# Two norms at the entry of the first FFN and of the SSD mixer: another order of weight splits, multiplications and additions

## The chip, the core and the metric

The kernel runs on one core of a Trainium2 chip. The metric is the device time of one execution, in microseconds (us). TensorE is called PE in the rows, VectorE DVE, ScalarE ACT, GpSimd POOL, SyncE SP.

## What is computed

Two layers over 256 context and 256 latent tokens of width 1024: the first has latent attention and a SwiGLU FFN, the second a bidirectional Mamba-2 (SSD) mixer and a SwiGLU FFN. Each of the four stands behind an RMS norm with modulation. What matters here is the entry of the first FFN and that of the SSD mixer:

```python
x = x + mod_x[2] * out_x
hx = rms_norm(x, norm_ffn[i]) * (1.0 + mod_x[4]) + mod_x[3]
x = x + mod_x[5] * swiglu(hx, ffn_w1[i], ffn_w3[i], ffn_w2[i])
...
def rms_norm(x, g):
    xf = x.astype(jnp.float32)
    y = xf * lax.rsqrt(jnp.mean(xf * xf, axis=-1, keepdims=True) + EPS)
    return (y * g.astype(jnp.float32)).astype(x.dtype)
```

The context tokens go through the same with their own modulation.

## The kernel before

**Layout.** The stream `X` ("residual") stands transposed: 1024 features as eight blocks k of 128 partitions, 512 tokens on the free axis, columns 0 to 255 the context, 256 to 511 the latent tokens (`HALF`). A matmul has a weight block as its stationary side and tokens as its moving side.

**Split numbers.** Each float32 operand of a matmul is cut into a high and a low half (fp32r), and a product is three matmuls: low tokens by high weights, high by high, high by low weights (lines 1776 to 1778). Weights come in blocks n of 128x1024. SyncE loads block n into one of four buffers `raw` once the low half of block n-4, which held the same buffer, has been made. `hi(n)` on ScalarE (L632) copies the raw block into `w_hi`, once the block is loaded and TensorE has used up block n-4, which held the same buffer . `lo(n)` on DVE (L1160) subtracts: `w_lo` = raw - `w_hi`; it waits for `w_hi`. The blocks have running numbers: `WO` the attention's output projection (8), `F0` the first FFN's w1 and w3, `G0` its w2 (three blocks an output tile, `g0(m)`), `BC` and what follows the SSD's input projection.

**Order.** Each engine runs its program in the order written; nothing is reordered. Semaphores join the engines. A wait stops all that is queued behind it on its engine.

**The two entries.** `norm_halves(w, n, ...)` exists twice, on ScalarE and on DVE, with w = 3 for the first FFN (called with n = F0 + 1) and w = 4 for the SSD mixer (n = BC + 1). It makes the norm and the operand for the context tokens first (half 0), then for the latent ones (half 1), while TensorE still ends the last tiles of the product before: in the first case output tiles 5, 6 and 7 of the projection (`SPLIT[3]`), in the second tile 7 of the FFN's w2 (`SPLIT[4]`), each done for the context columns first and for the latent columns afterwards. `add_half` (L1404) takes such a tile out of its PSUM bank: X = X + gate * bank. `square_half` (L662) squares it, POOL has summed the tiles before, and `half_sum` on TensorE (L1829, L1832) adds over the partitions with a matrix of ones. `rms_half` (L668) takes the square root, `inverse` (L1416) the reciprocal.

Of the operand's eight blocks k the even ones come as `value(h, k)` on DVE (L1424: X * gain * reciprocal), the high half with the shift on ScalarE (L677), and `low(h, k)` on DVE (L1434). The odd ones come from POOL (L502: X * reciprocal), ScalarE (L681 gain and shift, L683 high half) and `low(h, k)` (L1432). The buffers of `value` and of POOL hold two blocks each: value 4 waits for low 0's count, POOL's k = 5 for that of low 1, k = 7 for that of low 3.

TensorE takes the operand in four passes, of 48 matmuls each:

```python
def half_pair(w, n, outs, hh_, hl_, h):
    _, c0, c1 = HALF[h]
    pe.wait_ge(w_lo, n + 2)
    for k in range(KD):
        pe.wait_ge(h_lo, 8 * (2 * (w - 3) + h) + k + 1)
...
def four_halves(w, n, outs, hh_, hl_):
    half_pair(w, n, outs[0:2], hh_, hl_, 0)
    half_sum(w, 1)
    if w == 3:
        pe.wait_ge(added, 10)
    half_pair(w, n + 2, outs[2:4], hh_, hl_, 0)
    half_pair(w, n, outs[0:2], hh_, hl_, 1)
    half_pair(w, n + 2, outs[2:4], hh_, hl_, 1)
```

So the first pass wants blocks n and n+1 of the weights (F0 and F0+1, BC and BC+1), the second n+2 and n+3; `lo` of the first of them, F0 or BC, is made ahead of `norm_halves`. SyncE's first load of the FFN's following blocks waits for all sixteen low halves (`h_lo` 16), since vectors are loaded beside them into buffers that the norm uses.

Of the kernel before, what the change touches and what calls it, by code (L numbers as in the profile page):

```python
# [167 lines left out]
def late(t, k):  # L168

    return t >= k if isinstance(t, int) else True  # L170


def program(nc, a, out):
# [9 lines left out]
    with ExitStack() as fixed:  # L183
# [3 lines left out]
        def sem(name):  # L187
            return fixed.enter_context(nc.semaphore(name))
# [119 lines left out]
        w_hi, w_lo, w_used = sem("w_hi"), sem("w_lo"), sem("w_used")  # L308
# [312 lines left out]
        def _(act):  # L621
            A = nc.scalar.activation

            def hi(n, s):

                if isinstance(n, int) and n >= NBLK:
                    return
                act.wait_ge(raw_loaded[s % RING], 4 * (n - s % RING) + 16)
                if late(n, RING):
                    act.wait_ge(w_used, n - RING + 1)  # L630
                c = COLS[s]
                A(wh[s % RING][:, 0:c], raw[s % RING][:, 0:c], ACT.Copy).then_inc(w_hi, 1)  # L632
# [25 lines left out]
            def square_half(w, i, m, h, count):  # L658

                act.wait_ge(added, count)  # L660
                _, c0, c1 = HALF[h]
                A(T[:, SQ_AT[w, m], c0:c1], X[:, m, c0:c1], ACT.Square).then_inc(h_sq, 1)  # L662

            def rms_half(w, h):

                _, c0, c1 = HALF[h]
                act.wait_ge(h_sum, 2 * (w - 3) + h + 1)
                A(T[:, 4, c0:c1], bank[6 + h][:, 0:256], ACT.Sqrt, bias=eps[:, 0:1], scale=1.0 / D).then_inc(h_root, 1)  # L668

            def his_half(w, h, ks, hdst, gn, shift):  # L670

                m, c0, c1 = HALF[h]
                b = 2 * (w - 3) + h
                for k in ks:
                    if k % 2 == 0:
                        act.wait_ge(h_nv, 4 * b + k // 2 + 1)
                        A(hdst[:, k, c0:c1], T[:, 2 + k // 2 % 2, c0:c1], ACT.Identity, bias=shift(k, m)).then_inc(h_hi, 1)  # L677
                    else:
                        act.wait_ge(h_nx, 4 * b + k // 2 + 1)
                        v = T[:, 6 + k // 2 % 2, c0:c1]  # L680
                        A(v, v, ACT.Identity, bias=shift(k, m), scale=gn(k, m)).then_inc(h_odd, 1)  # L681
                        act.wait_ge(h_odd, 4 * b + k // 2 + 1)
                        A(hdst[:, k, c0:c1], v, ACT.Copy).then_inc(h_hi, 1)  # L683

            def norm_halves(w, n, base, hdst, gn, shift):

                S = len(SPLIT[w])
                for i, m in enumerate(SPLIT[w]):
                    square_half(w, i, m, 0, base + i + 1)
                hi(n, n)  # L690
                if S == 3:
                    square_half(w, 0, 5, 1, base + 4)
                rms_half(w, 0)
                his_half(w, 0, (0, 1), hdst, gn, shift)
                if S == 3:
                    square_half(w, 1, 6, 1, base + 5)
                hi(n + 1, n + 1)
                his_half(w, 0, (2, 3), hdst, gn, shift)
                square_half(w, S - 1, 7, 1, base + 2 * S)
                hi(n + 2, n + 2)  # L700
                his_half(w, 0, (4, 5, 6, 7), hdst, gn, shift)
                rms_half(w, 1)
                his_half(w, 1, range(KD), hdst, gn, shift)

# [189 lines left out]
            for m in range(5):  # L894
                hi(WO + m + RING, WO + m + RING)
                squares(3, m, 0, 0)
            norm_halves(3, F0 + 1, 5, H0h, lambda k, m: gain[1][:, k, m:m + 1], lambda k, m: mod[0][:, 24 + k, m:m + 1])

            def hidden(j, g, u, nt, U, n, s):
# [16 lines left out]
            for m in range(7):  # L916
                for n in range(g0(m), g0(m + 1)):
                    hi(n + RING, n + RING)
                squares(4, m, ADD1, 0)
            act.wait_ge(mod_done, 4)  # L920
            norm_halves(4, BC + 1, ADD1 + 7, H1h, lambda k, m: gain[2][:, k, m:m + 1], lambda k, m: mod[1][:, k, m:m + 1])
            act.wait_ge(up_zero, 4)

# [192 lines left out]
            for m in range(1, 8):  # L1116
                if m in (1, 2, 4, 5):
                    n = SO + 12 + (1, 2, 4, 5).index(m)
# [32 lines left out]
        def _(dve):  # L1151
            V = nc.vector

            def lo(n, s):

                if isinstance(n, int) and n >= NBLK:
                    return
                dve.wait_ge(w_hi, n + 1)
                c = COLS[s]
                V.tensor_tensor(wl[s % RING][:, 0:c], raw[s % RING][:, 0:c], wh[s % RING][:, 0:c].bitcast(f32), SUB).then_inc(w_lo, 1)  # L1160
# [239 lines left out]
            def add_half(ready, count, m, o, h, layer, chunk):  # L1400

                dve.wait_ge(ready, count)
                src, c0, c1 = HALF[h]
                V.scalar_tensor_tensor(X[:, m, c0:c1], o[:, 0:256], mod[layer][:, 8 * chunk + m, src:src + 1],  # L1404
                                       X[:, m, c0:c1], MUL, ADD).then_inc(added, 1)

            def norm_halves(w, n, base, lat_outs, used, gn, hdst, ldst, shift):

                S = SPLIT[w]
                layer, chunk = 0, 2 if w == 3 else 5  # L1410

                def inverse(h):

                    _, c0, c1 = HALF[h]
                    dve.wait_ge(h_root, 2 * (w - 3) + h + 1)
                    V.reciprocal(T[:, 5, c0:c1], T[:, 4, c0:c1]).then_inc(h_inv, 1)  # L1416
                    dve.wait_ge(h_inv, 2 * (w - 3) + h + 1)

                def value(h, k):

                    m, c0, c1 = HALF[h]
                    if k >= 4:
                        dve.wait_ge(h_lo, 8 * (2 * (w - 3) + h) + k - 3)
                    V.scalar_tensor_tensor(T[:, 2 + k // 2 % 2, c0:c1], X[:, k, c0:c1], gn(k, m), T[:, 5, c0:c1], MUL, MUL).then_inc(h_nv, 1)  # L1424

                def low(h, k):

                    m, c0, c1 = HALF[h]
                    dve.wait_ge(h_hi, 8 * (2 * (w - 3) + h) + k + 1)
                    hk = hdst[:, k, c0:c1].bitcast(f32)  # L1430
                    if k % 2:
                        V.tensor_tensor(ldst[:, k, c0:c1], T[:, 6 + k // 2 % 2, c0:c1], hk, SUB).then_inc(h_lo, 1)  # L1432
                    else:
                        V.scalar_tensor_tensor(ldst[:, k, c0:c1], T[:, 2 + k // 2 % 2, c0:c1], shift(k, m), hk, ADD, SUB).then_inc(h_lo, 1)  # L1434

                if len(S) == 3:
                    add_half(w_used, used, 5, lat_outs[0], 1, layer, chunk)
                dve.wait_ge(added, base + len(S))
                inverse(0)
                value(0, 0)  # L1440
                value(0, 2)
                if len(S) == 3:
                    add_half(w_used, used + 1, 6, lat_outs[1], 1, layer, chunk)
                low(0, 0)
                low(0, 1)
                lo(n, n)
                value(0, 4)
                low(0, 2)
                low(0, 3)
                lo(n + 1, n + 1)  # L1450
                add_half(w_used, used + 2, 7, lat_outs[-1], 1, layer, chunk)
                value(0, 6)
                low(0, 4)
                low(0, 5)
                lo(n + 2, n + 2)
                low(0, 6)
                low(0, 7)
                dve.wait_ge(added, base + 2 * len(S))
                inverse(1)
                value(1, 0)  # L1460
                for k in range(0, KD, 2):
                    if k + 2 < KD:
                        value(1, k + 2)
                    low(1, k)
                    low(1, k + 1)
# [8 lines left out]
            for i, m in enumerate(SPLIT[3]):  # L1474
                add_half(half_out, i + 1, m, bank[1 + i], 0, 0, 2)
            norm_halves(3, F0 + 1, 5, (bank[4], bank[5], bank[0]), WO + 6, lambda k, m: gain[1][:, k, m:m + 1],
                        H0h, H0l, lambda k, m: mod[0][:, 24 + k, m:m + 1])

# [24 lines left out]
            for m in range(7):  # L1503
# [9 lines left out]
                if m == 5:  # L1513
                    bias(1, 0, 48, VEC)
                    gains(2, 1, 1, "norm_mix", vec_bias, 4, 3)
                    gains(3, 1, 4, "norm_ffn", vec_bias, 4, 4)
            add_half(half_out, 4, 7, bank[1], 0, 0, 5)
            norm_halves(4, BC + 1, ADD1 + 7, (bank[2],), g0(7) + 1, lambda k, m: gain[2][:, k, m:m + 1],
                        H1h, H1l, lambda k, m: mod[1][:, k, m:m + 1])

# [927 lines left out]
```

## Time and profile before

| what | before |
|---|---|
| median of three runs | 1218.68 us (1218.53 to 1220.82) |
| time of the profiled execution | 1220.89 us |
| span of the profiled execution | 1219.1 us |
| PE busy | 1155.3 us (95%) |
| DVE busy | 866.8 us (71%) |
| ACT busy | 636.0 us (52%) |
| POOL busy | 216.4 us (18%) |

The span goes from the first to the last instruction; the time has in addition what lies around it, here 1.8 us. Busy shares are means over stages with different limits: PE is busy nearly always, and what it waits for at the entries of the stages is to be read there. Times in the rows are in us from the span's start.

### The profile page before, as it was taken

How to read it: one execution, taken by the hardware profiler on the slowest of the kernel's cores; microseconds unless marked ns; L12 is line 12 of the kernel's file. 1: busy time of each engine (PE TensorE's matmuls, PEld its weight loads, DVE VectorE, ACT ScalarE, POOL GpSimd, SP SyncE). 2: the span in 40 equal slices, each digit the busy share in tenths (PEclk: the TensorE clock that was granted, in tenths of full speed). 3: DMA queues.
4: the chain of work that ended last, by engine and by line, in shares of the span. 5: the costliest groups of instructions: out<-in, count | busy, mean ns of one | idle time of the engine just before them, and what ended most of it. 6: DMA issues, size and time to landing. Idle time of an engine off the chain costs nothing.

```text
span 1219.1 us, 19185 instructions
## 1 busy us (share of the span) xinstructions
PE 1155.3 (95%) x6954; PEld 968.7 (79%) x6954; DVE 866.8 (71%) x1320; ACT 636.0 (52%) x1078; POOL 216.4 (18%) x162
## 2 busy tenths in 40 slices
PE   5799999988999999999999899999999899999996
PEld 3577676668988888888888888887777799999996
DVE  0896889876687777776664688785788666767654
ACT  3646888644432223232222487567777356676742
POOL 0201445422100000000111200033965210000010
PEclk9899999999999999999999999999999899999999
DMA  9534132141375556546443132222212344555562
GB/s 379 203 122 138 53 104 87 36 163 45 125 256 185 177 189 206 170 178 208 144 160 123 53 130 87 82 76 85 66 58 69 105 139 157 174 171 175 167 213 65
DMA packets 48178, 168.27 MB, mean 138 GB/s; under 512 B 5232, under 2 KB 6512, under 8 KB 47856
## 3 DMA queue, kind: packets, MB, share of 16 engines
q1 hardware_dynamic: 48112, 167.38, 41.2%
q8 instruction: 42, 0.69, 0.2%
q14 instruction: 24, 0.20, 0.0%
HBM read 166.31 MB, written 1.05 MB: 137 GB/s over the span
## 4 chain that ended last, share of the span: by engine, by line
PE 73%; DVE 11%; ACT 6%; issue 6%; DMA 1%; SPq 1%; POOL 1%; DVEq 0%; ACTq 0%
PE bank L1776 21%; PE bank L1778 21%; PE bank L1777 21%; DVE w_lo L1160 3%; ACT w_hi L632 3%; PE bank L2212 2%; PE bank L2224 2%; DMA raw<-in_w_in 1%; PE bank L2245 1%; DVE softmax_max L1331 1%; PE bank L2234 1%; ACT L1135 1%; DVE mla_h_lo L1351 1%; PE bank L2139 1%; DVE vec_weights L1237 1%
## 5 line engine op out<-in xcount | busy, mean ns | idle before, releaser
L1160 DVE TENSOR_TENSOR w_lo<-raw,w_hi 128x1024 fp32r<-128x1024 f32 (+1 forms) x226 | 274.6, 1218 | 132.8 <-ACT w_hi L632 132.5
L632 ACT ACTIVATE w_hi<-raw 128x1024 fp32r<-128x1024 f32 (+1 forms) x226 | 230.2, 1021 | 243.3 <-PE bank L1778 219.2
L1776 PE MATMUL bank<-ffn_h_lo,w_hi 128*128 128x258 f32 (+2 forms) x736 | 246.1, 334 | 6.3 <-DVE ffn_h_lo L1434 2.8
L1778 PE MATMUL bank<-ffn_h_hi,w_lo 128*128 128x258 f32 (+2 forms) x736 | 244.3, 332 | 0.0
L1777 PE MATMUL bank<-ffn_h_hi,w_hi 128*128 128x258 f32 (+2 forms) x736 | 244.3, 332 | 0.0
L1776 PEld LDWEIGHTS bank<-ffn_h_lo,w_hi 128*128 128x128 f32 x736 | 139.3, 189 | 23.0 <-DVE ffn_h_lo L1434 3.3
L1777 PEld LDWEIGHTS bank<-ffn_h_hi,w_hi 128*128 128x128 f32 x736 | 139.1, 189 | 14.5
L1778 PEld LDWEIGHTS bank<-ffn_h_hi,w_lo 128*128 128x128 f32 x736 | 138.9, 189 | 14.7
L484 POOL TENSOR_TENSOR scratch<-scratch 128x512 f32<-128x512 f32 (+1 forms) x24 | 33.7, 1406 | 619.2 <-ACT scratch L641 619.2
L1776 PE MATMUL bank<-ssd_h_lo,w_hi 128*128 128x256 f32 (+2 forms) x360 | 125.7, 349 | 4.2 <-DVE ssd_h_lo L1434 2.3
L1776 PE MATMUL bank<-ffn_hidden_lo,w_hi 128*128 128x256 f32 (+1 forms) x374 | 123.4, 330 | 1.1 <-DVE ffn_hidden_lo L1730 0.9
L1778 PE MATMUL bank<-ffn_hidden_hi,w_lo 128*128 128x256 f32 (+1 forms) x374 | 123.1, 329 | 0.0
L1777 PE MATMUL bank<-ffn_hidden_hi,w_hi 128*128 128x256 f32 (+1 forms) x374 | 122.6, 328 | 0.0
L1777 PE MATMUL bank<-ssd_h_hi,w_hi 128*128 128x256 f32 (+2 forms) x360 | 117.3, 326 | 0.0
L1778 PE MATMUL bank<-ssd_h_hi,w_lo 128*128 128x256 f32 (+2 forms) x360 | 117.1, 325 | 0.0
L1535 DVE SCALAR_TENSOR_TENSOR scratch<-conv_in,par,scratch 128x512 f32<-128x512 f32 (+1 forms) x96 | 73.5, 767 | 18.4 <-ACT scratch L943 15.8
L1776 PEld LDWEIGHTS bank<-ssd_h_lo,w_hi 128*128 128x128 f32 (+1 forms) x360 | 68.0, 189 | 14.6 <-issue 3.9
L1776 PEld LDWEIGHTS bank<-ffn_hidden_lo,w_hi 128*128 128x128 f32 x374 | 70.3, 188 | 8.7 <-DVE ffn_hidden_lo L1730 1.1
L1777 PEld LDWEIGHTS bank<-ffn_hidden_hi,w_hi 128*128 128x128 f32 x374 | 70.7, 189 | 7.0
L1778 PEld LDWEIGHTS bank<-ffn_hidden_hi,w_lo 128*128 128x128 f32 x374 | 70.1, 188 | 7.0
L1777 PEld LDWEIGHTS bank<-ssd_h_hi,w_hi 128*128 128x128 f32 (+1 forms) x360 | 68.1, 189 | 9.4 <-issue 3.6
L1237 DVE SCALAR_TENSOR_TENSOR matvec_products<-scratch,silu_c_rows 128x1024 f32<-128x1024 f32 x56 | 73.8, 1317 | 0.0
(275 smaller groups left out, 2180.0 us busy)
## 6 DMA issues: line engine op xcount, KB each, us to landing
raw<-in_w SPq DMA_DIRECT2D x120, 512.0 KB, 4.4
scratch<-in_vec_w SPq DMA_DIRECT2D x56, 512.0 KB, 3.6
vec_weights<-in_vec_w SPq DMA_DIRECT2D x24, 512.0 KB, 3.6
raw<-in_w_xbc SPq DMA_DIRECT2D x24, 512.0 KB, 3.5
ada_start<-in_ada_w SPq DMA_DIRECT2D x8, 1024.0 KB, 17.2
raw<-in_w_z SPq DMA_DIRECT2D x16, 512.0 KB, 3.5
raw<-in_w_so SPq DMA_DIRECT2D x16, 512.0 KB, 3.5
raw<-in_w SPq DMA_DIRECT2D x16, 384.0 KB, 4.4
```

The source lines that it names most:

```text
L484: nc.gpsimd.tensor_tensor(T[:, ACC[w], 0:n], before, T[:, (b + k) % 2, 0:n], ADD).then_inc(sq_used, 2 if k == 1 else 1)
L632: A(wh[s % RING][:, 0:c], raw[s % RING][:, 0:c], ACT.Copy).then_inc(w_hi, 1)
L1135: A(T[:, u, 0:LAT], T[:, 6 + u, 0:LAT], ACT.Silu, bias=shift_out[:, u, 0:1]).then_inc(silu_done, 1)
L1160: V.tensor_tensor(wl[s % RING][:, 0:c], raw[s % RING][:, 0:c], wh[s % RING][:, 0:c].bitcast(f32), SUB).then_inc(w_lo, 1)
L1237: V.scalar_tensor_tensor(dst, buf, 1.0, crow[:, s, :], MUL, MUL, accum_out=m).then_inc(done, 1)
L1331: V.tensor_reduce(mx[:, c], bank[p][:, :], AX.X, ALU.max).then_inc(maxed, 1)
L1535: V.scalar_tensor_tensor(acc, up[:, u, seg, r:r + 256], par[:, PAR["conv_w"] + 5 * t + r:PAR["conv_w"] + 5 * t + r + 1], acc, MUL, ADD).th ...
L1776: mm(o, lh, rl, start=first, stop=False)
L1777: mm(o, lh, rh, start=False, stop=False)
L1778: return mm(o, ll, rh, start=False, stop=final)
L2212: last = mm(bank[6 + b][:, :], tabv(("gt", "lt")[d_]), mask_at(d_)[:, 4 * b:4 * b + 4, :], start=d_ == 0, stop=d_ == 1)
L2224: mm(bank[s // 2][:, :], Bt[:, tt, g, :], xsf[i % 6], start=s != 1, stop=s != 0).then_inc(st_mm, 1)
```

## The change

On ScalarE, the high half of weight block n+1 is made directly behind the square root of half 0, ahead of all high halves of the operand; that of n+2 behind the operand's k = 5; the squares of tiles 6 and 7 of half 1 stand later in the row of the operand's blocks (behind k = 3 and at the end). On DVE, the low half of block n is made ahead of the reciprocal; the operand's values 4 and 6 stand ahead of the additions of tiles 6 and 7 of half 1, the low half of block n+1 behind value 6, that of n+2 behind the last low half of the operand. Half 1 is left as it is. The block numbers are F0+1, F0+2, F0+3 in the first FFN and BC+1, BC+2, BC+3 in the SSD mixer; there, with `S == 1`, the additions and squares of tiles 5 and 6 don't exist. The same instructions run as before.

```diff
@@ ScalarE, norm_halves
                 rms_half(w, 0)
-                his_half(w, 0, (0, 1), hdst, gn, shift)
+                hi(n + 1, n + 1)
+                his_half(w, 0, (0, 1, 2, 3), hdst, gn, shift)
                 if S == 3:
                     square_half(w, 1, 6, 1, base + 5)
-                hi(n + 1, n + 1)
-                his_half(w, 0, (2, 3), hdst, gn, shift)
+                his_half(w, 0, (4, 5), hdst, gn, shift)
+                hi(n + 2, n + 2)
+                his_half(w, 0, (6, 7), hdst, gn, shift)
                 square_half(w, S - 1, 7, 1, base + 2 * S)
-                hi(n + 2, n + 2)
-                his_half(w, 0, (4, 5, 6, 7), hdst, gn, shift)
                 rms_half(w, 1)
@@ DVE, norm_halves
                 dve.wait_ge(added, base + len(S))
+                lo(n, n)
                 inverse(0)
                 value(0, 0)
                 value(0, 2)
-                if len(S) == 3:
-                    add_half(w_used, used + 1, 6, lat_outs[1], 1, layer, chunk)
                 low(0, 0)
                 low(0, 1)
-                lo(n, n)
                 value(0, 4)
                 low(0, 2)
                 low(0, 3)
+                if len(S) == 3:
+                    add_half(w_used, used + 1, 6, lat_outs[1], 1, layer, chunk)
+                value(0, 6)
                 lo(n + 1, n + 1)
-                add_half(w_used, used + 2, 7, lat_outs[-1], 1, layer, chunk)
-                value(0, 6)
                 low(0, 4)
                 low(0, 5)
-                lo(n + 2, n + 2)
+                add_half(w_used, used + 2, 7, lat_outs[-1], 1, layer, chunk)
                 low(0, 6)
                 low(0, 7)
+                lo(n + 2, n + 2)
```

## Rows read from the trace of the kernel before

**Rows 1.** Waits of PE from 298 us on, longest group: total, times, longest.

```profile
PE bank L1776 <- DVE w_lo L1160: 4.5, 3, 1.8
```

**Rows 2.** Timeline of PE, first FFN's entry: start, duration, line, operands, idle before.

```profile
294.87 0.28 PE L1778 MATMUL bank<-mla_h_hi,w_lo 128*128 128x256 f32 x1
...
297.71 0.28 PE L1778 MATMUL bank<-mla_h_hi,w_lo 128*128 128x256 f32 x1
298.97 0.39 PE L1776 MATMUL bank<-ffn_h_lo,w_hi 128*128 128x256 f32 x1 [0.98 <-DVE w_lo L1160]
...
304.42 0.39 PE L1776 MATMUL bank<-ffn_h_lo,w_hi 128*128 128x256 f32 x1 [2.35 <-DVE ffn_h_lo L1434]
...
306.83 0.58 PE L1776 MATMUL bank<-ffn_h_lo,w_hi 128*128 128x256 f32 x1 [0.41 <-DVE ffn_h_lo L1434]
...
309.48 0.59 PE L1829 MATMUL bank<-scratch,ones 128*128 128x256 f32 x2
...
311.02 0.47 PE L1776 MATMUL bank<-ffn_h_lo,w_hi 128*128 128x256 f32 x1
```

**Rows 3.** Timeline of DVE, context half of the same entry.

```profile
292.93 1.75 DVE L1416 RECIPROCAL scratch<-scratch 128x256 f32<-128x256 f32 x1 [1.82 <-ACT scratch L668]
294.72 1.94 DVE L1424 SCALAR_TENSOR_TENSOR scratch<-residual,gain,scratch 128x256 f32<-128x256 f32 x2
...
297.71 1.21 DVE L1160 TENSOR_TENSOR w_lo<-raw,w_hi 128x1024 fp32r<-128x1024 f32 x1
```

**Rows 4.** Timeline of ACT, context half of the same entry.

```profile
290.69 1.06 ACT L632 ACTIVATE w_hi<-raw 128x1024 fp32r<-128x1024 f32 x1 [1.96 <-PE bank L1778]
...
292.35 0.48 ACT L668 ACTIVATE scratch<-bank,eps 128x256 f32<-128x256 f32 x1 [0.30 <-PE bank L1832]
295.82 0.51 ACT L677 ACTIVATE ffn_h_hi<-scratch,mod 128x256 fp32r<-128x256 f32 x1 [2.99 <-DVE scratch L1424]
...
302.09 0.42 ACT L662 ACTIVATE scratch<-residual 128x256 f32<-128x256 f32 x1 [2.22 <-DVE residual L1404]
...
305.71 0.42 ACT L683 ACTIVATE ffn_h_hi<-scratch 128x256 fp32r<-128x256 f32 x1
```

**Rows 5.** Timeline of DVE, latent half of the same entry.

```profile
313.77 1.94 DVE L1424 SCALAR_TENSOR_TENSOR scratch<-residual,gain,scratch 128x256 f32<-128x256 f32 x2
...
316.35 0.43 DVE L1432 TENSOR_TENSOR ffn_h_lo<-scratch,ffn_h_hi 128x256 fp32r<-128x256 f32 x1 [0.24 <-ACT ffn_h_hi L683]
316.69 0.48 DVE L1424 SCALAR_TENSOR_TENSOR scratch<-residual,gain,scratch 128x256 f32<-128x256 f32 x1
317.09 0.96 DVE L1434 SCALAR_TENSOR_TENSOR ffn_h_lo<-scratch,mod,ffn_h_hi 128x256 fp32r<-128x256 f32 x1
```

**Rows 6.** Timeline of POOL, one multiplication of each half.

```profile
297.86 1.65 POOL L502 TENSOR_TENSOR scratch<-residual,scratch 128x256 f32<-128x256 f32 x1 [1.48 <-DVE ffn_h_lo L1432]
...
316.86 0.91 POOL L502 TENSOR_TENSOR scratch<-residual,scratch 128x256 f32<-128x256 f32 x1 [1.43 <-DVE ffn_h_lo L1432]
```

**Rows 7.** Timeline of PE, the SSD's entry.

```profile
678.55 0.39 PE L1776 MATMUL bank<-ssd_h_lo,w_hi 128*128 128x256 f32 x1 [1.77 <-DVE w_lo L1160]
...
684.00 0.38 PE L1776 MATMUL bank<-ssd_h_lo,w_hi 128*128 128x256 f32 x1 [2.34 <-DVE ssd_h_lo L1434]
...
688.75 0.59 PE L1829 MATMUL bank<-scratch,ones 128*128 128x256 f32 x2
```

**Rows 8.** Timelines of ACT and DVE, the SSD's entry.

```profile
671.05 1.06 ACT L632 ACTIVATE w_hi<-raw 128x1024 fp32r<-128x1024 f32 x1 [1.91 <-PE bank L1778]
...
672.57 1.75 DVE L1416 RECIPROCAL scratch<-scratch 128x256 f32<-128x256 f32 x1 [3.94 <-ACT scratch L668]
```

**Rows 9.** Busy us (instructions) by engine of two stretches; then granted PE clock, DMA.

```profile
304.40:309.40 5.00, 4.57 (x24) 4.17 (x25) 2.29 (x4) 1.70 (x4) 0.00 (x0) 0.66 0.00 0
...
684.00:688.70 4.70, 4.70 (x24) 4.42 (x25) 2.29 (x4) 1.68 (x4) 0.00 (x0) 0.64 0.35 119
```

**Rows 10.** Timeline of DVE, first split behind the first FFN's entry.

```profile
325.61 1.23 DVE L1160 TENSOR_TENSOR w_lo<-raw,w_hi 128x1024 fp32r<-128x1024 f32 x1 [4.68 <-ACT w_hi L632]
```

## The prediction

> **What bounds the kernel now.** I read the waits of TensorE first: behind 298 us the list is short, and at its head stands DVE's split of a weight block (w_lo), 4.5 us in three waits [rows 1]. In the two stages of the change TensorE waits for that and for DVE's low half of the operand (ffn_h_lo, ssd_h_lo) alone [rows 2, 7]. Then TensorE's own timeline through the first FFN's entry [rows 2]. Its last output-projection matmul starts at 297.71; the first FFN matmul stands 0.98 us later, released by w_lo (block F0+1); after four of eight k it waits 2.35 us for the low half of k=4, after k=6 another 0.41 us; the half sum of the latent tokens starts at 309.48 and the next pair at 311.02. From 306.83 on its timeline shows no wait before the SSD's entry at 678.55. So what is taken off this entry is kept: everything behind it hangs on TensorE, or on the operand that the entry makes. Behind the SSD's entry too the list has no wait for a split or an operand until the second FFN. The SSD's entry has the same waits, 1.77 and 2.34 us, and its half sum starts at 688.75 [rows 7].
>
> Why the low halves are late is read from DVE and ScalarE. DVE idles 1.82 us ahead of the first reciprocal and then puts the block F0+1 (1.21 us) between the low halves of k=1 and k=2 [rows 3]. ScalarE makes F0+1's high half already at 290.69, and idles 2.99 us ahead of the first high half at 295.82 [rows 4]. Two gaps stand ahead of the operand, and weights are made inside it.
>
> **The change part by part, first FFN.** No instruction is added or dropped; only orders change, on ScalarE and DVE. Nothing moves on SyncE or POOL, but their waits on w_lo and h_lo follow.
>
> *lo(F0+1) ahead of the reciprocal.* Its high half ends at 290.69 + 1.06 = 291.75; the split takes 1.21 us [rows 3], so until about 293.0. The reciprocal started at 292.93, after the square root at 292.35 + 0.48 [rows 3, 4]. Cost 0 to 0.1 us: the gap covers it. Without the gap it would cost 1.2. Queued behind it is everything of this half, and the square root's result waits with it.
>
> *hi(F0+2) behind the square root.* It needs the projection's tile m=6, whose last matmul ends at 294.87 + 0.28 = 295.15 [rows 2]. It runs about 295.25 to 296.20, where the first high half stood at 295.82 [rows 4]: that moves by 0.38 us, and the low halves with it. This is the one new cover that doesn't quite fit.
>
> *The order of the operand.* DVE now does value 0, 2, low 0, 1, value 4, low 2, 3, value 6, low 4, as it does already for the latent half; so I take the latent half's rhythm [rows 5]: from the first value low 1 starts at +2.58 (316.35 - 313.77), and low 2 ends 1.70 behind that start (317.09 + 0.96 - 316.35). With values at 294.72 as before and 0.38 for ScalarE: low 1 starts at 297.68, low 2 ends at 299.38, low 3 at 299.7. Ahead of low 4 then stand add_half (0.4), value 6 (0.4 alone, 0.9 beside a POOL multiplication), lo(F0+2) (1.2, with the start of the next inside it 1.1) and low 4 itself (0.48): 299.7 + 0.4 + 0.9 + 1.1 + 0.5 = 302.6.
>
> *What TensorE sees.* A matmul is 0.118 us (24 of them from 294.87 to 297.71), one k of a pair of tiles is six, 0.71 us [rows 2]; a start after a wait costs 0.1 more. F0+1 is there at 293, low 0 at 297.2, so the pair starts at 297.83 instead of 298.97. k=2 waits 0.2 (low 2 at 299.38), k=4 would start at 300.95 and waits 1.6 until 302.6. Thereafter ScalarE decides: the square, hi(F0+3) and four high halves, the same six pieces as now from 302.09 to 305.71 + 0.42, take 4.04 us [rows 4], now from 300.15: 304.2. Low 7 is done at 304.65 and TensorE reaches k=7 at 304.8: no further wait. The pair ends and the half sum starts at 305.5; before 309.48. **Gain 4.0 us.** Of it about 1.2 is the clock: before, the stretch 304.4 to 309.4 has a granted mean of 0.66 [rows 9], a part of it at 1.2 instead of 2.4 GHz, right behind the 2.35 us wait; from 306.83 the two k left would have taken 1.5 at the full clock, to 308.3.
>
> *lo(F0+3) at the end.* It now ends after low 7, near 305.8; the second pair needs it when the half sum is done, 305.5 + 1.54 = 307.0 (309.48 to 311.02). Margin 1.2 us, cost nothing. The square of m=7 ends at 304.5, a microsecond ahead of the half sum. From there on all is as before, 4.0 us earlier. SyncE's next weight load waits for the last low half of the latent half, which follows the half sum; its split starts at 325.61 [rows 10] and ends at 326.8, and TensorE asks for it after 144 matmuls from 311.02, at 328.1: 1.3 us of slack, unchanged as both move alike.
>
> **The SSD's entry.** Here hi(BC+1) ends later, 671.05 + 1.06, so lo(BC+1) holds DVE to 673.3 and the reciprocal moves from 672.57 by 0.72 us [rows 8]. hi(BC+2) is done at 675.8, ahead of the first high half, now at 676.2. With the same rhythm from values at 675.08: low 0 ends at 677.41, low 1 at 678.09, low 2 at 679.37, low 3 at 679.70. There is no add_half ahead of value 6, so value 6 ends DVE's work at 680.0, then lo(BC+2) 1.1 and low 4: 681.6, or 682.1 with 0.5 us lost to POOL. TensorE starts at 677.5 instead of 678.55, waits 0.44 for k=2 and 0.7 to 1.2 for k=4, and ends the pair at 684.6 to 685.1; before, 688.75 [rows 7]. **Gain 3.6 to 4.1, I take 3.9.** About 0.9 of it is clock (684 to 688.7 has 0.64 [rows 9]; the waits of k=6 hide the rest). lo(BC+3) ends at 684.3 to 684.8, needed about 685.5.
>
> The unknown in both is POOL: beside its multiplication DVE's operation of 0.48 took 0.96, and POOL's own 0.91 became 1.65 behind a split [rows 5, 6]. How many of the moved operations are hit isn't seen; between none and two for each half, 0 to 1.0 us a stage, and I put in one. The Trainium skill (SBUF — State Buffer, section "SBUF: two separate sides") says that DVE and GpSimd hold their shared ports exclusively, and that the one that comes second waits for the whole of the other's instruction. The rows agree in kind: 0.96 is 0.48 more. By that rule a split that comes second could lose most of POOL's instruction, as an estimate 0.4 us a stage more than I took, and the sum would be 7.1 instead of 7.9.
>
> **Sum**: 4.0 + 3.9 = 7.9 us, against the profiled execution: its span of 1219.1 to 1211.2, its time of 1220.89 to 1213.0. The median of the timed runs is 1218.68, 2.2 below the profiled one. If that is the low clock not falling there (1.2 + 0.9 by the above), the gain against the median is 5.8 and the time 1212.9; if it is something else, 1218.68 - 7.9 = 1210.8.
>
> **Rivals.** *The clock falls all the same.* Waits of 1.6 us, and 0.44 and about 1 us, remain inside the first pair. Against it: the 1.77 us wait at 678.55 was followed by matmuls at the full clock, and both falls stand behind 2.35 and 2.34 us. For it: the waits now come close together. It would cost at least the 0.9 to 1.2 of before and at most 24 matmuls at half clock, 2.8, in each stage; at 1.2 each 1215.4, with the gain against a median without the fall down to 3.3. The Trainium skill (TensorE: Matmul & The Clock Gate, section "A second HAM failure mode: psum-queue depth-cycling") says that frequent short idles between groups of matmuls make the clock swing between its two levels. That speaks for this rival, and the 1.77 us wait against it.
>
> *The wait moves instead of going.* The splits still stand ahead of low 4 and low 6. If add_half, value 6, the split and low 4 are each stretched beside POOL, or hi(n+1) holds ScalarE longer than 0.38, low 4 comes when it did (304.4) and only one stage gains: 1220.9 - 4 = 1216.9, no change that can be told. Against it: POOL has only two multiplications there.
>
> *Slower: lo(n+2) becomes the bound.* It now stands at the very end, behind add_half of m=7 and low 7, and TensorE's second pair stops for it. It decides from 1.2 us of delay on; to be slower than now it must end after 311.0 instead of 305.8, some 5 us of stretching, ten DVE operations by 0.5. With both stages hit by 6 us the time is about 1222.5. POOL's two multiplications give no more than 1.8, so it gets little.
>
> **How the numbers follow.** Forecast 1213.0, chance 0.72; the clock falls all the same, 0.13, 1215.4; the wait moves, 0.10, 1216.9; slower, 0.05, 1222.5. The range goes from 1210.6 (the median less 7.9, and no POOL delay) to 1216.9. This kernel's measurement tells about 0.2%, 2.4 us, from no change: faster is below 1216.2, slower above 1221.1. Faster 0.83 (the forecast and nearly all of the clock's case), same 0.12, slower 0.05.
>
> **What would show it.** Right: TensorE's first FFN matmul directly behind the projection's last one, its first wait at k=4 below 2 us, half sums 3.5 to 4.2 us earlier relative to the projection, lo(F0+1) ending where the reciprocal starts, the SSD's reciprocal 0.7 later relative to its square root, no low clock behind the pair. Wrong: a wait for w_lo at the second pair, a wait at k=4 over 2.3 us, or a new wait behind the entry that takes the gain back, first at the next weight block, where 1.3 us of slack stand.

## The result and the profile after

| what | before | after |
|---|---|---|
| median of the runs beside each other | 1219.83 us (1218.53 to 1220.82) | 1214.23 us (1211.81 to 1214.32) |
| ratio, 95% interval | | 0.9946 (0.9934 to 0.9958) |
| profiled execution: span | 1219.1 us | 1212.4 us |
| PE busy | 1155.3 us | 1152.0 us |
| first FFN: half sum of the context tokens to that of the latent ones | 19.05 us | 15.11 us |
| SSD: the same | 17.96 us | 14.44 us |
| from the first FFN's second half sum to the SSD's first | 361.31 us | 361.32 us |

The ratio says 6.6 us of 1219.8 (5.1 to 8.1); the two medians alone differ by 5.6. The last three lines are differences of start times: the first matmul of a half sum marks where the last tile has just been squared, the second where the first pass over the operand has ended. 3.94 us went at the first entry, 3.52 at the second, and nothing came back between them.

TensorE's timeline through the first FFN's entry, after (columns as before: start, duration, line, operation, idle before):

```profile
298.57 0.28 PE L1778 MATMUL bank<-mla_h_hi,w_lo 128*128 128x256 f32 x1
298.70 0.28 PE L1776 MATMUL bank<-ffn_h_lo,w_hi 128*128 128x256 f32 x1
...
303.29 0.39 PE L1776 MATMUL bank<-ffn_h_lo,w_hi 128*128 128x256 f32 x1 [1.28 <-DVE ffn_h_lo L1434]
...
306.40 0.59 PE L1829 MATMUL bank<-scratch,ones 128*128 128x256 f32 x2
...
307.94 0.47 PE L1776 MATMUL bank<-ffn_h_lo,w_hi 128*128 128x256 f32 x1
```

This profile stands 0.86 us later than that of before already ahead of the change (the projection's last matmul is at 298.57 instead of 297.71). The pair follows the projection directly, where 0.98 us stood [rows 2]; one wait of 1.28 us stands at k=4 instead of 2.35, none at k=6; the half sum is at 306.40 - 0.86 = 305.5.

DVE in the same stretch, after:

```profile
292.71 1.23 DVE L1160 TENSOR_TENSOR w_lo<-raw,w_hi 128x1024 fp32r<-128x1024 f32 x1 [0.73 <-ACT w_hi L632]
293.85 1.75 DVE L1416 RECIPROCAL scratch<-scratch 128x256 f32<-128x256 f32 x1
...
299.30 0.96 DVE L1434 SCALAR_TENSOR_TENSOR ffn_h_lo<-scratch,mod,ffn_h_hi 128x256 fp32r<-128x256 f32 x1
...
300.91 0.78 DVE L1424 SCALAR_TENSOR_TENSOR scratch<-residual,gain,scratch 128x256 f32<-128x256 f32 x1
301.62 1.21 DVE L1160 TENSOR_TENSOR w_lo<-raw,w_hi 128x1024 fp32r<-128x1024 f32 x1
...
305.45 1.22 DVE L1160 TENSOR_TENSOR w_lo<-raw,w_hi 128x1024 fp32r<-128x1024 f32 x1
```

The split of F0+1 fills the gap of 1.82 us [rows 3], and the reciprocal starts at 293.85 - 0.86 = 292.99, 0.06 later than before. Low 2 and value 6 are stretched beside POOL (0.96, 0.78 us). Two splits now stand at 301.62 and 305.45, the second behind the operand.

The SSD's entry, after: DVE, then POOL, then TensorE.

```profile
669.14 1.23 DVE L1160 TENSOR_TENSOR w_lo<-raw,w_hi 128x1024 fp32r<-128x1024 f32 x1 [3.58 <-ACT w_hi L632]
670.29 1.75 DVE L1416 RECIPROCAL scratch<-scratch 128x256 f32<-128x256 f32 x1
...
677.00 1.76 DVE L1160 TENSOR_TENSOR w_lo<-raw,w_hi 128x1024 fp32r<-128x1024 f32 x1
```

```profile
676.76 0.93 POOL L502 TENSOR_TENSOR scratch<-residual,scratch 128x256 f32<-128x256 f32 x1 [0.70 <-DVE ssd_h_lo L1432]
```

```profile
674.55 0.36 PE L1776 MATMUL bank<-ssd_h_lo,w_hi 128*128 128x256 f32 x1 [0.84 <-DVE ssd_h_lo L1434]
...
676.40 0.39 PE L1776 MATMUL bank<-ssd_h_lo,w_hi 128*128 128x256 f32 x1 [0.18 <-DVE ssd_h_lo L1434]
...
679.22 0.39 PE L1776 MATMUL bank<-ssd_h_lo,w_hi 128*128 128x256 f32 x1 [1.13 <-DVE ssd_h_lo L1434]
...
682.16 0.59 PE L1829 MATMUL bank<-scratch,ones 128*128 128x256 f32 x2
```

The waits for w_lo are gone (1.77 us before [rows 7]); the operand is waited for three times, 2.15 us in all, against once, 2.34 us, before. The split of BC+2 took 1.76 us instead of 1.2: POOL's multiplication of k=7 had begun at 676.76.

The granted clock behind these waits, after: busy us and instructions by engine (PE, weight loads, DVE, ACT, POOL), then clock and DMA, as in [rows 9].

```profile
303.20:308.00 4.80, 4.71 (x33) 4.43 (x33) 2.80 (x6) 2.15 (x5) 0.00 (x0) 1.00 0.00 0
679.20:683.00 3.80, 3.78 (x29) 3.71 (x29) 2.56 (x5) 0.81 (x2) 0.00 (x0) 1.00 0.56 143
```

Both are at the full clock, where before it was at 0.66 and 0.64.

### The profile page after: what moved, and what is told of

It is laid out like the page before. It is cut to its first block, busy times and chain, and to the rows that moved or that the text cites. A ratio compares the mean times of both kernels' runs of the same rounds, so it can differ in the third digit from the quotient of the medians.

```text
span 1212.4 us, 19185 instructions
## 1 busy us (share of the span) xinstructions
PE 1152.0 (95%) x6954; PEld 965.5 (80%) x6954; DVE 867.5 (72%) x1320; ACT 635.9 (52%) x1078; POOL 213.3 (18%) x162
## 4 chain that ended last, share of the span: by engine, by line
PE 73%; DVE 11%; ACT 6%; issue 6%; DMA 1%; SPq 1%; POOL 1%; DVEq 0%; ACTq 0%
PE bank L1776 21%; PE bank L1778 21%; PE bank L1777 21%; DVE w_lo L1160 3%; ACT w_hi L632 3%; PE bank L2212 2%; PE bank L2224 2%; DMA raw<-in_w_in 1%; PE bank L2245 1%; DVE softmax_max L1331 1%; PE bank L2234 1%; ACT L1135 1%; DVE mla_h_lo L1351 1%; PE bank L2139 1%; DVE vec_weights L1237 1%
```

## The experiments

The theory: TensorE's waits inside the first pass of each entry are what the change saves, and behind the entries the gain is carried unchanged. Its rivals: the clock is most of it; one of the two moved things alone, the weights or the order, is; the late split gives it back. In the table are the two half-sum distances of each profiled execution and the time against the kernel before, from runs on the same chip.

| kernel | first FFN | SSD | ratio of times (95%) |
|---|---|---|---|
| before | 19.05 | 17.96 | 1 |
| after (first comparison) | 15.11 | 14.44 | 0.9946 (0.9934 to 0.9958) |
| after_again | 15.11 | 14.43 | 0.9948 (0.9935 to 0.9961) |
| ffn_only | 15.11 | 17.91 | 0.9973 (0.9964 to 0.9983) |
| ssd_only | 18.56 | 14.43 | 0.9973 (0.9963 to 0.9983) |
| weights_only | 18.15 | 17.69 | 0.9986 (0.9978 to 0.9995) |
| order_only | 16.52 | 15.62 | 0.9969 (0.9958 to 0.9980) |
| lo2_early | 15.76 | 15.28 | 0.9958 (0.9944 to 0.9971) |
| before_fill | 17.93 | 17.15 | 1.0001 (0.9993 to 1.0010) |
| operand_first | 13.23 | 13.24 | 0.9917 (0.9904 to 0.9930) |

From the first FFN's second half sum to the SSD's first, every one of them has 361.31 or 361.32 us.

### One entry at a time

```diff
 def norm_halves(w, n, ...):        # on ScalarE and on DVE
+    if w == 3:                     # ffn_only; w == 4 for ssd_only
+        ...the order after
+    else:
+        ...the order before
```

> The change at the first FFN's entry alone, the SSD's entry as before. Theory (the change takes TensorE's waits off each entry's first pair, independently): the half sum of the latent tokens at the first FFN comes 4.0 us earlier, the SSD's first pair keeps its waits of 1.8 and 2.3 us, and the time falls by about 3.5 to 4.0 us (ratio about 0.997). Rival (one entry carries it all, or the earlier work is given back at the next entry): 0 or the whole 6.6.

> The change at the SSD's entry alone, the first FFN's entry as before. Theory: the SSD's half sum comes 3.5 us earlier relative to the FFN's last tile, the first FFN keeps its 0.98 and 2.35 us waits, and the time falls by about 3 to 3.5 us (ratio about 0.997); with the first entry alone it adds up to the whole. Rival: 0 or the whole 6.6.

Each entry gives what it gives in the whole change (15.11, 14.43), and the other stays as it was but for the clock: in ssd_only the first FFN has 18.56 instead of 19.05, with the same waits of 0.98 and 2.35 us, but the granted clock is low from 304.5 to 307.7, and the wait of 0.41 us at k=6 is gone. The times fall by 0.27% each, 3.3 us, and 3.3 + 3.3 is the whole of 6.6. The entries are independent.

### The weights alone, the order alone

weights_only (ScalarE, then DVE):

```diff
                 rms_half(w, 0)
+                hi(n + 1, n + 1)
                 his_half(w, 0, (0, 1), hdst, gn, shift)
                 if S == 3:
                     square_half(w, 1, 6, 1, base + 5)
-                hi(n + 1, n + 1)
...
                 dve.wait_ge(added, base + len(S))
+                lo(n, n)
                 inverse(0)
...
                 low(0, 1)
-                lo(n, n)
```

> Half of the change at both entries: block n's low half ahead of the reciprocal and block n+1's high half behind the square root, while squares, additions and the block n+2 keep their places. Theory (the end of the first pair is set by the low halves of k=4 to 7, not by its start): TensorE starts the pair 1 us earlier but waits longer, 2.5 to 2.9 us, at k=4, since ScalarE still squares tile 7 and makes n+2's high half ahead of k=4; worked out, low 4 comes 0.7 us earlier at the FFN and 0.35 at the SSD, and the gain is 1 to 2.5 us in all. Rival (the early start is the gain): 2.2 us for the two starts, and with the operand's waits gone up to 6.6.

order_only, against the changed kernel (ScalarE, then DVE):

```diff
-                hi(n + 1, n + 1)
-                his_half(w, 0, (0, 1, 2, 3), hdst, gn, shift)
+                his_half(w, 0, (0, 1), hdst, gn, shift)
+                hi(n + 1, n + 1)
+                his_half(w, 0, (2, 3), hdst, gn, shift)
...
-                lo(n, n)
                 inverse(0)
...
                 low(0, 1)
+                lo(n, n)
...
+                lo(n + 2, n + 2)
                 low(0, 6)
                 low(0, 7)
-                lo(n + 2, n + 2)
```

> The other half at both entries: the operand's values 4 and 6 ahead of the additions and the squares behind k=3 and at the end, while block n's low half stays between the low halves of k=1 and k=2, block n+1's high half behind k=1 and block n+2's low half ahead of k=6. Theory: the pair starts as before, its wait at k=4 falls from 2.35 to about 1.3 us, one at k=6 of 0.8 stays, the pair ends 1.4 us earlier at the FFN without the clock's share and 2.6 with it, and the gain is 3 to 5 us in all. Rival (the weights in the gap are the gain): below 1.5 us.

The weights alone take 0.90 and 0.27 us off the two distances, the order alone 2.53 and 2.34. In weights_only the k=4 of the pair starts 13.23 and 12.86 us behind the first half sum instead of 13.99 and 13.21, so 0.76 and 0.35 earlier, as expected. Why the early start is worth little is seen on ScalarE and TensorE of weights_only:

```profile
300.37 0.42 ACT L662 ACTIVATE scratch<-residual 128x256 f32<-128x256 f32 x1 [2.02 <-DVE residual L1404]
300.69 1.04 ACT L632 ACTIVATE w_hi<-raw 128x1024 fp32r<-128x1024 f32 x1
301.64 0.49 ACT L677 ACTIVATE ffn_h_hi<-scratch,mod 128x256 fp32r<-128x256 f32 x1
```

```profile
302.70 0.39 PE L1776 MATMUL bank<-ffn_h_lo,w_hi 128*128 128x256 f32 x1 [2.53 <-DVE ffn_h_lo L1434]
```

ScalarE idles 2.02 us for the addition of tile 7, squares it, copies a weight block, and only then makes the high half of k=4; TensorE, started a microsecond earlier, waits 2.53 us there. The start was not what set the end. Together the two halves give more (3.94 and 3.52) than their sum (3.43 and 2.61): once the operand comes in time, the early start counts in full.

### The last split put back

```diff
                 add_half(w_used, used + 2, 7, lat_outs[-1], 1, layer, chunk)
+                lo(n + 2, n + 2)
                 low(0, 6)
                 low(0, 7)
-                lo(n + 2, n + 2)
```

> The changed kernel with one piece undone: block n+2's low half stands ahead of the low half of k=6 again instead of behind that of k=7. Theory (low 6 and low 7 end the first pair): low 6 comes 1.0 to 1.1 us later, TensorE waits 0.7 to 0.9 us for it at both entries, and the kernel loses 1.4 to 1.6 of the 6.6 us (ratio 0.9957 to 0.996). Rival (block n+2 at the very end bounds the second pair, so moving it forward helps or is free): 0 or a gain.

The distances grow by 0.65 and 0.84 us, with a wait of 0.58 and 0.57 at k=6 that the changed kernel doesn't have; the time has 0.9958 against 0.9946 and 0.9948, in the expected direction and size. The intervals overlap, and this profile has a stretch of low clock behind the entries (771 to 775 us) that those of the changed kernel don't have, so the distances show it and the times alone would not. The last split behind the operand costs nothing, and the rival "slower" has no footing: the second pass never waits for w_lo.

### The changed kernel once more

> The changed kernel once more, beside the others on the same chip. Theory: ratio 0.9946, the half sums of the latent tokens 15.1 and 14.4 us behind those of the context tokens. Rival: a ratio that differs by more than 0.002 would say that the first comparison was disturbed.

The same to 0.01 us in the distances and 0.0002 in the ratio.

### The clock by itself

```diff
 def half_pair(w, n, outs, hh_, hl_, h, fill=False):
     for k in range(KD):
+        if fill and k == 4:
+            for _ in range(16):
+                mm(bank[7][:, 0:256], wh[n % RING][:, 0:128], hh_[:, 0, c0:c1], start=True, stop=True)
         pe.wait_ge(h_lo, 8 * (2 * (w - 3) + h) + k + 1)
```

Only the first of the four passes is called with `fill`.

> The kernel before, with sixteen idle matmuls (1.9 us, into a bank that nobody reads until the next half sum overwrites it) in TensorE's wait ahead of k=4 at both entries; every low half, split and addition stays where it was. It measures the clock's share alone. Theory: the granted clock no longer falls behind the two waits, the half sums of the latent tokens come 1.2 us earlier at the first FFN and 0.9 at the SSD, and the time falls by up to 2.1 us, less where the clock of the kernel before doesn't fall in every execution (ratio 0.998 to 0.9995). Rival (the clock is most of the gain): 4 us or more. Rival (the clock is nothing): 0.

In its profile the clock no longer falls at the entries (1.00 from 303.70 to 307.70, and from 682.20 to 686.10 too), the operand comes when it did, and the distances shrink by 1.12 and 0.81 us: this is what the low clock costs there. Yet the time doesn't move: 1.0001 (0.9993 to 1.0010), so at most 0.9 us of gain where the two distances show 1.9. Two readings of its windows:

```profile
303.70:307.70 4.00, 3.38 (x25) 3.06 (x26) 2.30 (x5) 1.73 (x4) 0.00 (x0) 1.00 0.00 0
...
770.00:780.00 10.00, 10.00 (x55) 8.64 (x54) 6.55 (x8) 3.36 (x5) 0.00 (x0) 0.83 0.25 66
```

In this execution the clock fell at 775 us instead, in the middle of the SSD's convolutions, where TensorE shows no idle time at all; behind the second half sum this execution is 1.3 us longer than that of before (531.6 against 530.35). Either the falls at the entries aren't in most executions of the kernel before, or others come in their place. The mean granted clock that is on record for each run speaks for the second: it is 0.985 to 0.988 in the 45 runs of the kernel before beside the experiments (0.987 in its profile, which has both falls), and 0.986 to 0.990, 0.988 in the mean, in before_fill's eleven; seven of the ten runs of the changed kernel, in whose profiles the clock doesn't fall at the entries, have 0.991. So the time of before_fill doesn't price the falls at the entries; its distances do, at 1.9 us of the 7.46 that the change takes off them. With that the rival "the clock is most of it" is out, but the clock's share is not nothing: in most runs of the changed kernel no others come in their place (the other three of its ten have 0.989).

What the clock is worth in time is seen within weights_only: its six runs with 0.991 took 1217.1 to 1218.4 us, its six with 0.985 to 0.988 took 1218.7 to 1220.4, and the means lie 1.9 us apart. So the ratio of weights_only, too, is in part the clock's. Where the clock stood low in runs without a profile isn't on record.

### A step further

```diff
 # ScalarE
                 rms_half(w, 0)
+                his_half(w, 0, range(KD), hdst, gn, shift)
+                if S == 3:
+                    square_half(w, 1, 6, 1, base + 5)
+                hi(n + 1, n + 1)
+                square_half(w, S - 1, 7, 1, base + 2 * S)
+                hi(n + 2, n + 2)
 # DVE: lo(n), reciprocal, values and low halves 0 to 5 as in the latent half, then
+                if len(S) == 3:
+                    add_half(w_used, used + 1, 6, lat_outs[1], 1, layer, chunk)
+                low(0, 6)
+                low(0, 7)
+                add_half(w_used, used + 2, 7, lat_outs[-1], 1, layer, chunk)
+                lo(n + 1, n + 1)
+                lo(n + 2, n + 2)
 # TensorE, second pass
-                half_pair(w, n + 2, outs[2:4], hh_, hl_, 0)
+                for i in range(2):
+                    pe.wait_ge(w_lo, n + 3 + i)
+                    ...the eight k of tile outs[2 + i]
```

> A step further: of the weights only block n is made ahead of the operand; the low halves of n+1 and n+2 both stand behind low 7, their high halves on ScalarE behind the operand's last high half, and TensorE's second pass takes its two tiles one after the other, so that the first needs block n+1... that is, its third weight block alone. Theory (the remaining waits of 1.3 and 1.1 us at k=4 come from the split and the addition ahead of low 4): the first FFN's pair runs without a wait and ends 2.0 us earlier than in the changed kernel, the SSD's 1.3 us earlier, the second pass finds its weights (0 to 0.3 us of wait), and the time falls by another 3 us (ratio about 0.992). Rival (the split that is put off comes back as a wait of the second pass): a wait for w_lo of 1 us or more there, and a ratio of 0.994 or above.

The distances are 13.23 and 13.24 us, another 1.88 and 1.19 off, and the time 0.9917 (0.9904 to 0.9930), 10 us below the kernel before and some 3.5 below the changed one. TensorE's waits of this kernel from 298 to 690 us (total, times, longest) and the start of its second pass:

```profile
PE bank L1774 <- DVE ssd_h_lo L1432: 1.0, 2, 0.8
```

```profile
303.19 0.59 PE L1827 MATMUL bank<-scratch,ones 128*128 128x256 f32 x2
...
304.73 0.47 PE L1774 MATMUL bank<-ffn_h_lo,w_hi 128*128 128x256 f32 x1
```

The first FFN's entry has no wait left; the SSD's has those of 0.84 and 0.19 us at its start, which hang on the reciprocal behind the split. The splits that were put off don't come back as a wait.

## Why the prediction was right

*Bound and carry.* That the gain of an entry is kept rested on TensorE having no wait behind it [rows 2, 7]. The 361.31 or 361.32 us between the two entries in nine kernels show it to a hundredth for the first entry. Behind the SSD's second half sum 530.0 to 530.4 us are left in seven of the ten profiles; the other three, with 531.6 to 531.7 (order_only, lo2_early, before_fill), each have a stretch of low clock there.

*First FFN, forecast 4.0 us, measured 3.94.* The steps hold one by one: the split in the gap cost 0.06 (0 to 0.1 forecast); the pair starts directly behind the projection; the first high half moved from 295.82 [rows 4] to 297.08 - 0.86 = 296.2, by 0.4 (0.38 forecast); the wait at k=4 was 1.28 instead of 1.6, in part since value 6 held DVE for 0.71 us beside POOL (300.91 to 301.62) and not for 0.9; the half sum came at 305.5 as written; the second pass started 1.54 behind it, without a wait. The clock's part of the gain, 1.2 here and 0.9 at the SSD by forecast, is 1.12 and 0.81 by before_fill.

*SSD, forecast 3.9 between 3.6 and 4.1, measured 3.52.* The term that was mis-sized is POOL's. I put the pair's end between no stretched operation and one (684.6 to 685.1) and took the middle; the split beside POOL's k=7 did take 0.55 more, and the end came a tenth behind the upper end: 682.16 + 3.07 = 685.2 in the times of before (3.07 is 671.05 - 667.98, ScalarE's copy of BC+1 in both profiles). So the gain fell a little short of the range. The split, started second at 677.00, lost 0.55 of the 0.69 us that POOL's multiplication still ran (676.76 + 0.93 = 677.69). No run moves that multiplication away; order_only, where the same two meet, has 1.75 us for the split. The Trainium skill (SBUF — State Buffer, section "SBUF: two separate sides") says that the one that starts first holds the shared ports for its whole instruction. The trace agrees with that in kind; the estimate of 7.1 for the sum that was made by it was somewhat low, as 3.94 + 3.52 = 7.46, and my 7.9 somewhat high.

*Sum and time.* 7.9 was forecast between profiled executions; the spans differ by 6.7, which is 7.46 less the 0.86 by which the profile after was later already ahead of the entries, to a tenth. Against the median I gave 5.8 if the clock falls rarely in the timed runs, 7.9 if not; the measured 6.6 lies between, and its interval, 5.1 to 8.1, holds both. The step on the clock was the weak one: that the timed runs sit 2.2 us below the profiled one because the low clock was absent there isn't borne out. The 45 runs of before have the profile's granted clock to 0.002 and times from 1218.3 to 1222.5, so the profiled 1220.89 is an ordinary one and the median of three, 1218.68, was a low one; the ten profiles differ by up to 2.0 us already where the first half sum starts (289.3 to 291.3). The forecast of 1213.0 was taken from the profiled run, 1.1 above the median of 1219.83, and that it lies within 1.2 us of the measured median is in part luck.

*The rivals.* The clock did not fall behind the remaining waits of 1.28 and 1.13 us in either profile of the changed kernel; three of its ten runs have a mean clock of 0.989 instead of 0.991, and where it was low in them isn't known. But my evidence against that rival, a 1.77 us wait followed by the full clock [rows 7], doesn't hold in general: in order_only the same wait of 1.78 us was followed by the low clock (mean 0.62 from 675.6 to 680.1), and there it hid behind the wait for low 4. The wait did not move instead of going, and the last split did not become the bound (lo2_early).

## What to carry to other kernels

Where an engine waits for an operand made in slices, look at what stands between the slices on each engine of the chain: here additions and squares for the next half, and weights that were needed much later, cost more than the late start that the list of waits put first. Place such work by when its reader asks for it, ahead of the chain where an engine idles or behind its last slice, and change both ends together: the early start alone gave 1.2 us of 7.5, as TensorE then waited in the middle. An idle gap is worth filling only up to when its input comes: the split ahead of the SSD's reciprocal held it back by 0.8 us (1.34 behind the start of the square root instead of 0.56), as its high half came late.

## What was unexpected of the hardware

The granted clock fell in stretches where TensorE showed no idle time: 0.83 over 770 to 780 us in before_fill, with 10.00 of 10.00 us busy by the profile, where the kernel before has 1.00; lo2_early shows the same at 766 to 776. And a wait of the same length was followed by the low clock in one execution (1.78 us, order_only) and not in two others (1.77 us, before; 1.78 us, before_fill). In weights_only one and the same kernel has a mean granted clock of 0.991 in six runs and of 0.985 to 0.988 in six. Nothing here settles what decides it.
